# Two pairs of pieces per group in seven products, and four of eight low parts by an accumulating transfer

## The chip, the cores and the metric

One core of one Trainium2 chip runs the whole program. The metric is the device time of one execution in microseconds (us), given as the median of several runs.

## What is computed

Two transformer blocks are applied to 256 tokens of width 2048, all in f32. The change touches only the last stage, the feed-forward of the second block. Cut to that:

```python
hn = rms_norm_2(h, norm_ffn_g)
gate, up = jnp.split(hn @ w_gate_up, 2, axis=-1)     # each 5632 wide
h = h + (jax.nn.silu(gate) * up) @ w_down            # 5632 x 2048
...
return rms_norm_2(h, norm_final_g)
```

## The kernel before

**Pieces.** All weights are streamed from HBM in pieces of two k-tiles of 128 rows by 512 columns (512 KB in SBUF). SyncE loads two pieces with one transfer of 1 MB (L417) into one of four slots of `raw` (`RAWS` = 4). Each f32 weight is split into two parts of type float32r, because a product is made of three: high by high, high by low, low by high. ScalarE rounds the high part into `hi` (L577), VectorE subtracts it from the raw weights and writes the low part into `lo` (L941). `hi` and `lo` have four slots (`RING` = 4). So the split of piece n waits until TensorE has used piece n-4 (`pieces_used`, L574 and L940). In the order of their programs ScalarE and VectorE run three pieces ahead of TensorE (`AHEAD` = 3, `split_to` in `walk`, L496), and there the splits are interleaved with the evacuation of the groups and with other steps. SyncE waits before each load until the low parts of both pieces of the slot are made (`lo_ready`, L405).

**The last stage.** It is written out in three chunks: `f2_up0`, `f2_down0`, `f2_up1`, `f2_down1`, `f2_up2`, `f2_down2` (`ffn`, L134). An up segment computes gate and up products and writes their product, split in two parts, into `B` as tokens (`token_parts`, L368). A down segment multiplies `B` by `w_down` in four groups of 512 output columns. A group has 8 pieces in `f2_down0` and `f2_down1`, and 6 in `f2_down2`. The evacuation of a group (`tpart`, `tlast`, L1170) adds two PSUM banks to the residual `HT`. An ordinary piece of a down group is 12 matmuls of 512 columns (`piece`, L1594, L1616 to L1618).

**Seven products.** In 11 of the 12 down groups pieces 2 and 3 (`SEVEN_AT` = 2, `seven_product_pairs`, L203) are computed by a scheme with seven block products instead of eight: 42 matmuls of 256 columns (`seven_products`, L1751, L1757 to L1759). It needs sums of weight blocks and of activation blocks:

- `block_sums` (L949), in VectorE's program behind the low part of the piece before the pair: four operations, L957 to L961, of which L959 changes the raw weights in place. ScalarE's high part of the pair's first piece waits for it (`t1_set`, L576).
- `t_hi` (ScalarE, L584) and `t_lo` (VectorE, L945), the two parts of the block sums, both behind the split of the pair's second piece.
- `activation_sums` (L976), behind the up group of turn 1 of each up segment (L523): four additions on VectorE (L980 to L983), a copy on ScalarE (L595), a subtraction on VectorE (L987), into `s_form`.
- `combine` (L964): ScalarE copies a product (L589) and VectorE makes five operations (L969 to L974). It runs in the middle of the group, three pieces behind the pair (L520), and adds to `HT`. The group's evacuation (L1174) adds the rest.

GpSimd issues small loads in the first 30 us and nothing after them (L441 to L484).

Of the kernel before, what the change touches and what calls it, by code (L numbers as in the profile page):

```python
# [19 lines left out]
ALU = mybir.AluOpType  # L20
# [25 lines left out]
TOKEN_AT = 16  # L46
# [203 lines left out]
def bass_two_blocks(nc, ins, out):  # L250
    SEGS, TOTAL = schedule()
    PAIRS = seven_product_pairs(SEGS)

    with ExitStack() as ctx:
# [6 lines left out]
        def overlay(**shapes):  # L261
# [19 lines left out]
        s_form, t_sum = overlay(s_form=([P, 2, 4, 2, P], F32R), t_sum=[P, 2, 3, SEVEN_COLS])  # L281
# [8 lines left out]
        small = sb("small", [P, 64])  # L290
        r_fin = sb("r_fin", [P, T])
# [18 lines left out]
        _, t_hi, t_lo = overlay(gfin_end=[P, MT * T + 3 * D], t_hi=([P, 2, 3, SEVEN_COLS], F32R), t_lo=([P, 2, 3, SEVEN_COLS], F32R))  # L310
# [30 lines left out]
            sem("first_block_sums_set"), sem("block_sums_set"), sem("block_sums_hi"), sem("block_sums_lo"), sem("block_sums_used"))  # L341
        s_ready, p1_copied = sem("activation_sums_ready"), sem("first_product_copied")
# [38 lines left out]
        def _(sp):  # L381
# [114 lines left out]
        def walk(eng, tallies, split, evacuate, side, each_turn, combine, activation_sums, last):  # L496
# [5 lines left out]
            for seg in SEGS:  # L502
                def run(turn, t):
# [10 lines left out]
                    for g, kind in enumerate(seg.kinds):  # L514
                        G = turn * len(seg.kinds) + seg.g0 + g
                        for j in range(seg.pieces):
# [3 lines left out]
                            if t is not None and j == SEVEN_AT + 3 and base + g * seg.pieces + SEVEN_AT in PAIRS:  # L520
                                combine(PAIRS[base + g * seg.pieces + SEVEN_AT], b0, turn * len(seg.kinds) + g)
                            if j == seg.pieces - 1:
                                sums = seg.name.startswith("f2_up") and kind == "up" and t == SEVEN_AT // 2  # L523
                                left = [MORE.get(kind, 0) + sums]

                                def more():
# [5 lines left out]
                                         token_parts if seg.name.startswith("f2") else B_parts)  # L532
                                if sums:
                                    activation_sums(more)
# [18 lines left out]
        def _(act):  # L553
# [12 lines left out]
            def split(n, slot):  # L566
# [8 lines left out]
                if isinstance(n, int) and n in PAIRS:  # L575
                    act.wait_ge(t1_set, PAIRS[n] + 1)  # L576
                act.activation(hi[:, slot % RING], raw[:, raw_slot, 2 * (slot % 2):2 * (slot % 2) + 2, :],  # L577
                               ACT.Copy).then_inc(hi_ready, 1)
                if isinstance(n, int) and n - 1 in PAIRS:
                    q = PAIRS[n - 1]  # L580
# [5 lines left out]
            def combine(q, b0, gi):  # L586
# [4 lines left out]
            def activation_sums(more):  # L591
                more()
                asked.skip()
                wait(asked)
                given.mark(act.activation(s_form[:, 0], pb_copy[:, :, :].rearrange("p f (i c) -> p f i c", i=2), ACT.Copy))  # L595
# [25 lines left out]
            def evacuate(kind, G, end, b0, gi, k, more, to_b):  # L621
# [294 lines left out]
            walk(act, {1: asked, 2: given, 3: ready}, split, evacuate, side, lambda quarter, turn: None, combine, activation_sums, last)  # L916
# [3 lines left out]
        def _(dve):  # L920
# [14 lines left out]

            def split(n, slot):

                dve.wait_ge(hi_ready, n + 1)
                if not isinstance(n, int) or n >= RING:
                    dve.wait_ge(pieces_used, n - RING + 1)  # L940
                dve.tensor_tensor(lo[:, slot % RING], raw[:, slot // 2 % RAWS, 2 * (slot % 2):2 * (slot % 2) + 2, :],  # L941
                                  hi[:, slot % RING], ALU.subtract).then_inc(lo_ready, 1)
                if isinstance(n, int) and n - 1 in PAIRS:
                    dve.wait_ge(t_hi_ready, PAIRS[n - 1] + 1)
# [4 lines left out]
            def block_sums(n):  # L949

                w = raw[:, n // 2 % RAWS, :, :].rearrange("p (i e) (s c) -> p i e s c", e=2, s=2)
                dve.wait_ge(raw_landed[n // 2 % RAWS], landed(n // 2))
                dve.wait_ge(h_turned, 16)
                if PAIRS[n]:
                    dve.wait_ge(t_lo_ready, PAIRS[n])
# [6 lines left out]
                dve.wait_ge(t1_set, PAIRS[n] + 1)  # L962

            def combine(q, b0, gi):  # L964

                x = HT[:, :, gi * GC:(gi + 1) * GC]
# [9 lines left out]
            def activation_sums(more):  # L976
# [10 lines left out]
                dve.tensor_tensor(s_form[:, 1], pb_copy[:, :, :].rearrange("p f (i c) -> p f i c", i=2), s_form[:, 0],  # L987
# [32 lines left out]
            def evacuate(kind, G, end, b0, gi, k, more, to_b):  # L1020
# [149 lines left out]
                elif kind in ("tpart", "tlast"):  # L1170
# [3 lines left out]
                    dve.tensor_tensor(x, x, ps[:, b0:b0 + 2, :], ALU.add).then_inc(psum_free, 1)  # L1174
# [343 lines left out]
            walk(dve, {0: own, 1: asked, 2: given, 3: ready}, split, evacuate, side, turn_h, combine, activation_sums, last)  # L1518
# [3 lines left out]
        def _(pe):  # L1522
# [71 lines left out]
            def piece(seg, g, j, slot, b0, n, steps=None):  # L1594
# [3 lines left out]
                if isinstance(n, int) and n == 0:  # L1598
                    pe.wait_ge(first_lo, 1)
                else:  # L1600
                    pe.wait_ge(lo_ready, n + 1)
                for kk in range(2):
                    k = 2 * j + kk + (4 * WIDEST_FIRST[g] if seg.name == "pool" else 0)
                    first = j == 0 and kk == 0
                    final = (j == seg.pieces - 1 or isinstance(n, int) and n == TOTAL - RING - 1) and kk == 1
# [145 lines left out]
            def seven_products(j, slot, b0, n):  # L1751

                Xh, Xl = token_parts
                half = SEVEN_COLS

# [8 lines left out]
                def summed(f, i):  # L1764
                    return s_form[:, 0, f, i, :], s_form[:, 1, f, i, :]
# [9 lines left out]
                pe.wait_ge(s_ready, PAIRS[n] // 4 + 1)  # L1775
                for i in range(2):
                    k = 2 * (j + i)
                    pe.wait_ge(lo_ready, n + i + 1)
                    product(p16[:, 0:half], i == 0, False, tokens(0, k), *block(0, 0, i))
                    product(z0[:, 0:half], False, False, tokens(0, k + 1), *block(1, 0, i))  # L1780
                    product(z0[:, half:GC], False, False, summed(3, i), *block(1, 1, i))
                    product(p57[:, 0:half], i == 0, False, summed(0, i), *block(0, 1, i)).then_inc(pieces_used, 1)
                pe.wait_ge(t_lo_ready, PAIRS[n] + 1)
                for i in range(2):
                    k = 2 * (j + i)
                    product(p16[:, half:GC], False, i == 1, summed(1, i), *block_sum(1, i))
                    product(p57[:, half:GC], False, i == 1, summed(2, i), *block_sum(0, i))
                    last = product(z1[:, 0:half], False, False, tokens(1, k + 1), *block_sum(2, i))
# [24 lines left out]
            for seg in SEGS:  # L1813
                def run(turn, t):
                    for g, kind in enumerate(seg.kinds):
# [10 lines left out]
                        for j in range(seg.pieces - RING if at_end else seg.pieces):  # L1826
# [9 lines left out]
                            if isinstance(n, int) and n in PAIRS:  # L1836
                                seven_products(j, slot, b0, n)
# [47 lines left out]
```

## Time and profile before

| | |
|---|---|
| median of 3 runs | 2616.38 us (2616.24 to 2616.57) |
| the profiled execution, its own time | 2616.46 us |
| its span, first to last instruction | 2614.7 us |
| granted TensorE clock, mean | 0.999 |
| TensorE busy | 2602.3 us, 21534 matmuls |
| VectorE busy, ScalarE busy | 1694.6 us, 1187.4 us |
| DMA, mean over the span | 193 GB/s, 504.31 MB |

Times in the rows are microseconds from the start of the span. PE is TensorE (PEld its weight loads), DVE is VectorE, ACT ScalarE, POOL GpSimd, SP SyncE; a name with q behind it is an engine's queue. L12 is line 12 of the kernel. Matmuls overlap, so the distance between the starts of two matmuls is what one costs, not its own duration.

### The profile page before, as it was taken

What the parts mean: (1) busy time and instruction counts of PE and PEld (TensorE: products, weight loads), DVE (VectorE), ACT (ScalarE), POOL (GpSimd) and SP (SyncE); (2) the same over time, 40 slices, a digit from 0 to 9 for tenths busy, and PEclk for the clock granted to TensorE, in tenths of its full rate; (3) what the DMA queues carried; (4) which work ended last, traced back from release to release, by engine and by line L of the source; (5) the groups of instructions that cost most, each with busy time, mean ns of one, the idle gap of its engine ahead of it and who ended that gap; (6) DMA issues with size and microseconds to landing.
All of it is one profiled execution on the core that took longest, in us unless ns stands there. A gap on an engine that the chain in (4) does not pass through costs nothing.

```text
span 2614.7 us, 50642 instructions
## 1 busy us (share of the span) xinstructions
PE 2602.3 (100%) x21534; PEld 2551.2 (98%) x21534; DVE 1694.6 (65%) x1817; ACT 1187.4 (45%) x1284; POOL 14.6 (1%) x33
## 2 busy tenths in 40 slices
PE   9999999999999999999999999999999999999998
PEld 8989999999999999999999999999999989998997
DVE  7668765555555556795676666556777875677567
ACT  5356554434443444465443433444544444444444
POOL 2000000000000000000000000000000000000000
PEclk9999999999999999999999999999999999999999
DMA  9654566565655565555555555555565555556553
GB/s 306 202 168 163 196 193 196 187 201 187 200 186 200 188 199 193 179 203 195 180 184 189 193 182 190 193 193 194 193 210 194 193 198 193 191 195 205 194 179 129
DMA packets 254461, 504.31 MB, mean 193 GB/s; under 512 B 9390, under 2 KB 11456, under 8 KB 254160
## 3 DMA queue, kind: packets, MB, share of 16 engines
q1 hardware_dynamic: 250160, 496.27, 56.8%
q10 hardware_dynamic: 3136, 4.21, 0.5%
q8 instruction: 131, 2.15, 0.3%
q0 software_dynamic: 992, 1.34, 0.2%
q14 instruction: 42, 0.34, 0.0%
HBM read 498.89 MB, written 2.89 MB: 192 GB/s over the span
## 4 chain that ended last, share of the span: by engine, by line
PE 99%; DVE 1%; issue 0%; ACT 0%; POOL 0%; DVEq 0%; ACTq 0%; POOLq 0%
PE ps L1579 49%; PE ps L1590 25%; PE ps L1637 4%; PE ps L1646 4%; PE ps L1641 3%; PE ps L1616 3%; PE ps L1618 3%; PE ps L1617 3%; PE ps L1757 1%; PE ps L1759 1%; PE ps L1758 1%; PE ps L1626 1%; PE ps L1627 1%; PE ps L1624 1%; DVE lo L941 0%
## 5 line engine op out<-in xcount | busy, mean ns | idle before, releaser
L941 DVE TENSOR_TENSOR lo<-raw,hi 128x1024 fp32r<-128x1024 f32 x939 | 1139.7, 1224 | 792.6 <-ACT hi L577 779.2
L577 ACT ACTIVATE hi<-raw 128x1024 fp32r<-128x1024 f32 x939 | 988.4, 1059 | 1208.0 <-PE ps L1590 924.3
L1579 PE MATMUL ps<-A,hi 128*128 128x256 f32 x7286 | 902.8, 276 | 0.0
L1579 PEld LDWEIGHTS ps<-A,hi 128*128 128x128 f32 x7286 | 861.1, 188 | 0.3
L1579 PE MATMUL ps<-B,hi 128*128 128x256 f32 x3963 | 491.0, 276 | 0.0
L1590 PE MATMUL ps<-A,lo 128*128 128x256 f32 x3648 | 487.7, 276 | 0.0
L1579 PEld LDWEIGHTS ps<-B,hi 128*128 128x128 f32 x3963 | 468.3, 188 | 0.1
L1590 PEld LDWEIGHTS ps<-A,lo 128*128 128x128 f32 x3648 | 447.5, 188 | 0.0
L1590 PE MATMUL ps<-B,lo 128*128 128x256 f32 x1984 | 265.2, 276 | 0.0
L1590 PEld LDWEIGHTS ps<-B,lo 128*128 128x128 f32 x1984 | 243.3, 188 | 0.0
L1637 PE MATMUL ps<-B,hi 128*128 128x260 f32 (+3 forms) x768 | 109.1, 284 | 0.0
L1646 PE MATMUL ps<-B,lo 128*128 128x258 f32 (+3 forms) x768 | 108.7, 284 | 0.0
L1641 PE MATMUL ps<-B,hi 128*128 128x256 f32 x768 | 104.1, 278 | 0.0
L1637 PEld LDWEIGHTS ps<-B,hi 128*128 128x128 f32 x768 | 100.0, 189 | 0.0
L1646 PEld LDWEIGHTS ps<-B,lo 128*128 128x128 f32 x768 | 98.9, 189 | 0.0
L1616 PE MATMUL ps<-hi,B 128*128 128x512 f32 x248 | 96.8, 390 | 0.0
L1618 PE MATMUL ps<-hi,B 128*128 128x512 f32 x248 | 96.6, 389 | 0.0
L1617 PE MATMUL ps<-lo,B 128*128 128x512 f32 x248 | 96.5, 389 | 0.0
L1641 PEld LDWEIGHTS ps<-B,hi 128*128 128x128 f32 x768 | 96.3, 188 | 0.0
L676 ACT ACTIVATE B<-work 128x1024 f32 (+1 forms) x26 | 27.6, 1063 | 72.5 <-DVE work L1081 64.6
L1618 PEld LDWEIGHTS ps<-hi,B 128*128 128x128 f32 x248 | 46.5, 188 | 10.0
L1617 PEld LDWEIGHTS ps<-lo,B 128*128 128x128 f32 x248 | 46.6, 188 | 9.2
(306 smaller groups left out, 1589.5 us busy)
## 6 DMA issues: line engine op xcount, KB each, us to landing
raw<-in_w_in_dram SPq DMA_DIRECT2D x135, 1024.0 KB, 5.1
raw<-in_ffn_w_dram SPq DMA_DIRECT2D x132, 1024.0 KB, 5.1
raw<-in_w_gate_up_dram SPq DMA_DIRECT2D x88, 1024.0 KB, 5.0
raw<-in_w_down_dram SPq DMA_DIRECT2D x44, 1024.0 KB, 5.0
raw<-in_w_out_dram SPq DMA_DIRECT2D x16, 1024.0 KB, 5.1
raw<-in_pl_w_gate_dram SPq DMA_DIRECT2D x16, 1024.0 KB, 5.1
raw<-in_conv_out_w_dram SPq DMA_DIRECT2D x16, 1024.0 KB, 5.0
raw<-in_w_o_dram SPq DMA_DIRECT2D x16, 1024.0 KB, 5.0
```

Source lines behind the costliest of these rows:

```text
L577: act.activation(hi[:, slot % RING], raw[:, raw_slot, 2 * (slot % 2):2 * (slot % 2) + 2, :], ACT.Copy).then_inc(hi_ready, 1)
L676: given.mark(act.activation(some((A_parts if kind == "cb" else to_b)[0], k, 4, 0, T), work[:, :, :], ACT.Copy))
L941: dve.tensor_tensor(lo[:, slot % RING], raw[:, slot // 2 % RAWS, 2 * (slot % 2):2 * (slot % 2) + 2, :], hi[:, slot % RING], ALU.subtract). ...
L1579: pe.matmul(ps[:, b0 + m, 0:T], high(slot, kk, m), x, start=j == 0 and kk == 0 and part == 0, stop=False)
L1590: last = pe.matmul(ps[:, b0 + m, 0:T], low(slot, kk, m), Xh, start=False, stop=j == seg.pieces - 1 and kk == 1)
L1616: pe.matmul(to, Xh, hi[:, slot % RING, kk, :], start=first, stop=False)
L1617: pe.matmul(to, Xh, lo[:, slot % RING, kk, :], start=False, stop=False)
L1618: last = pe.matmul(to, Xl, hi[:, slot % RING, kk, :], start=False, stop=final)
L1624: pe.matmul(to, Wh, Xh, start=first and m % 2 == 0, stop=False, skip_group_check=True)
L1637: pe.matmul(ps[:, b0 + m, 0:with_lo], high(slot, kk, m), B[:, 2 * j + kk, 0:with_lo], start=first and kk == 0, stop=False, skip_group_chec ...
L1641: pe.matmul(ps[:, b0 + m, 0:T], high(slot, kk, m), B_low[:, 2 * j + kk, :], start=False, stop=False, skip_group_check=True)
L1646: last = pe.matmul(ps[:, b0 + m, 0:with_hi], low(slot, kk, m), B[:, 2 * j + kk, 0:with_hi], start=False, stop=final and kk == 1, skip_grou ...
```

## The change

- Pieces 6 and 7 of the 8-piece groups also become a pair in seven products, so that there are 19 pairs instead of 11. The first products of both pairs gather in the same PSUM banks, and `combine` moves from the middle of the group into its evacuation, where it also takes over the addition of the two plain banks.
- The low parts of pieces 0, 1, 4 and 5 of these groups, and of pieces 0 and 1 of the first three groups of `f2_down2`, 38 in all, are no longer made by VectorE. ScalarE writes the negative high part into `lo` with a second activation (scale -1), and GpSimd then issues a transfer that adds the raw weights to it (`accum_op`). TensorE waits for the transfer (`low_landed`), and so does SyncE before it loads over the raw slot.
- `activation_sums` also runs behind the up group of turn 3 in `f2_up0` and `f2_up1`; `s_form` gets a second half.
- Addresses: the tokens in `B` start at column 0 instead of 16, `t_hi` and `t_lo` lie 48 elements further, `t_sum` moves from the place of `h` to another, and `block_sums` no longer waits for `h_turned`.

The diff, cut to its core:

```diff
-TOKEN_AT = 16
+TOKEN_AT = 0
...
-SEVEN_AT = 2
+PAIRS_AT = {"f2_down0": (2, 6), "f2_down1": (2, 6), "f2_down2": (2,)}
+LOWS_BY_DMA_AT = {"f2_down0": (0, 1, 4, 5), "f2_down1": (0, 1, 4, 5), "f2_down2": (0, 1)}
+SUMS_BEHIND = {"f2_up0": (1, 3), "f2_up1": (1, 3), "f2_up2": (1,)}
...
+def down_groups(segs):
+
+
+    return [(x, x.p0 + turn * x.per_turn + g * x.pieces)
+            for x in segs if x.name in PAIRS_AT for turn in range(2) for g in range(2)][:-1]
+
+
 def seven_product_pairs(segs):
 
 
-    first = [x.p0 + turn * x.per_turn + g * x.pieces + SEVEN_AT
-             for x in segs if x.name.startswith("f2_down") for turn in range(2) for g in range(2)]
-    return {n: q for q, n in enumerate(first[:-1])}
+
+    pairs, groups = {}, {}
+    for i, (x, first) in enumerate(down_groups(segs)):
+        for u, j in enumerate(PAIRS_AT[x.name]):
+            pairs[first + j] = (len(pairs), sum(len(PAIRS_AT[f"f2_down{c}"]) for c in range(int(x.name[-1]))) + u, u)
+        groups[first] = (i, len(pairs) - 1)
+    return pairs, groups
+
+
+def lows_by_dma(segs):
+
+
+    count, turns = {}, [0] * RING
+    for x, first in down_groups(segs):
+        for j in LOWS_BY_DMA_AT[x.name]:
+            turns[(first + j) % RING] += 1
+            count[first + j] = turns[(first + j) % RING]
+    return count
...
-        s_form, t_sum = overlay(s_form=([P, 2, 4, 2, P], F32R), t_sum=[P, 2, 3, SEVEN_COLS])
+        s_form, = overlay(s_form=([P, 2, 2, 4, 2, P], F32R))
...
+        t_sum, = overlay(t_sum=[P, 2, 3, SEVEN_COLS])
...
-        _, t_hi, t_lo = overlay(gfin_end=[P, MT * T + 3 * D], t_hi=([P, 2, 3, SEVEN_COLS], F32R), t_lo=([P, 2, 3, SEVEN_COLS], F32R))
+        _, t_hi, t_lo = overlay(gfin_end=[P, MT * T + 3 * D + 48], t_hi=([P, 2, 3, SEVEN_COLS], F32R), t_lo=([P, 2, 3, SEVEN_COLS], F32R))
...
-                                sp.wait_ge(lo_ready, n * 2 - 2 * RAWS + 2)
+                                if isinstance(n, int) and 2 * (n - RAWS) in LOWS_BY_DMA:
+                                    for m in (2 * (n - RAWS), 2 * (n - RAWS) + 1):
+                                        sp.wait_ge(low_landed[m % RING], 16 * LOWS_BY_DMA[m])
+                                else:
+                                    sp.wait_ge(lo_ready, n * 2 - 2 * RAWS + 2)
...
+            for i, n in enumerate(LOWS_BY_DMA):
+                pool.wait_ge(low_begun, i + 1)
+                pool.dma_start(lo[:, n % RING].bitcast(F32), raw[:, n // 2 % RAWS, 2 * (n % 2):2 * (n % 2) + 2, :],
+                               accum_op=ALU.add).then_inc(low_landed[n % RING], 16)
...
-                            if t is not None and j == SEVEN_AT + 3 and base + g * seg.pieces + SEVEN_AT in PAIRS:
-                                combine(PAIRS[base + g * seg.pieces + SEVEN_AT], b0, turn * len(seg.kinds) + g)
                             if j == seg.pieces - 1:
-                                sums = seg.name.startswith("f2_up") and kind == "up" and t == SEVEN_AT // 2
+                                behind = SUMS_BEHIND.get(seg.name, ())
+                                sums = kind == "up" and t in behind
+                                seven = SEVEN_GROUPS.get(base + g * seg.pieces) if t is not None else None
...
                 act.activation(hi[:, slot % RING], raw[:, raw_slot, 2 * (slot % 2):2 * (slot % 2) + 2, :],
                                ACT.Copy).then_inc(hi_ready, 1)
+                if isinstance(n, int) and n in LOWS_BY_DMA:
+                    act.activation(lo[:, slot % RING], raw[:, raw_slot, 2 * (slot % 2):2 * (slot % 2) + 2, :],
+                                   ACT.Copy, scale=-1.0).then_inc(low_begun, 1)
...
-            def evacuate(kind, G, end, b0, gi, k, more, to_b):
+            def evacuate(kind, G, end, b0, gi, k, more, to_b, seven):
+                if seven:
+                    combine(*seven, b0)
...
+                if isinstance(n, int) and n in LOWS_BY_DMA:
+                    passed[0] += 1
+                else:
+                    dve.wait_ge(hi_ready, n + 1)
+                    if not isinstance(n, int) or n >= RING:
+                        dve.wait_ge(pieces_used, n - RING + 1)
+                    dve.tensor_tensor(lo[:, slot % RING], raw[:, slot // 2 % RAWS, 2 * (slot % 2):2 * (slot % 2) + 2, :],
+                                      hi[:, slot % RING], ALU.subtract).then_inc(lo_ready, 1 + passed[0])
+                    passed[0] = 0
...
-                dve.wait_ge(h_turned, 16)
...
+            def combine(c, q, b0, x):
+
                 p1, v5, v7, u2 = (work[:, i, :] for i in range(4))
-                dve.wait_ge(p1_copied, q + 1)
+                dve.wait_ge(t_used, q + 1)
+                own.mark(dve.tensor_tensor(x, x, ps[:, b0:b0 + 2, :], ALU.add))
+                dve.wait_ge(p1_copied, c + 1)
                 step(dve.tensor_tensor(u2, p1, ps[:, b0 + 2, SEVEN_COLS:GC], ALU.add))
                 step(dve.tensor_tensor(work[:, 1:3, :], row_of(u2, 2), ps[:, b0 + 3, :].rearrange("p (s c) -> p s c", s=2), ALU.add))
-                dve.tensor_tensor(x[:, 0, :], x[:, 0, :], work[:, 0:2, :].rearrange("p s c -> p (s c)"), ALU.add)
+                own.mark(dve.tensor_tensor(x[:, 0, :], x[:, 0, :], work[:, 0:2, :].rearrange("p s c -> p (s c)"), ALU.add))
                 x1 = x[:, 1, :].rearrange("p (s c) -> p s c", s=2)
                 step(dve.tensor_tensor(x1, x1, row_of(v7, 2), ALU.add))
-                step(dve.tensor_tensor(x[:, 1, SEVEN_COLS:GC], x[:, 1, SEVEN_COLS:GC], ps[:, b0 + 3, 0:SEVEN_COLS], ALU.add))
-
-            def activation_sums(more):
+                return dve.tensor_tensor(x[:, 1, SEVEN_COLS:GC], x[:, 1, SEVEN_COLS:GC], ps[:, b0 + 3, 0:SEVEN_COLS], ALU.add)
...
+                    if seven:
+                        combine(*seven, b0, x).then_inc(psum_free, 1)
+                    else:
+                        dve.tensor_tensor(x, x, ps[:, b0:b0 + 2, :], ALU.add).then_inc(psum_free, 1)
...
+                elif isinstance(n, int) and n in LOWS_BY_DMA:
+                    pe.wait_ge(low_landed[n % RING], 16 * LOWS_BY_DMA[n])
                 else:
                     pe.wait_ge(lo_ready, n + 1)
...
+                q, sums, u = PAIRS[n]
+                closes = j == seg.pieces - 2
+                last_pair = u == 1 or n + 4 not in PAIRS
...
-                pe.wait_ge(s_ready, PAIRS[n] // 4 + 1)
+                pe.wait_ge(s_ready, sums + 1)
```

## Rows read from the trace of the kernel before

**Rows 1.** The page's first part: busy time of each engine
```profile
PE 2602.3 (100%) x21534; PEld 2551.2 (98%) x21534; DVE 1694.6 (65%) x1817; ACT 1187.4 (45%) x1284; POOL 14.6 (1%) x33
```

**Rows 2.** Whom TensorE waited for, 1900 to 2615 us: total, times, longest
```profile
PE ps L1757 <- DVE lo L941: 2.8, 2, 2.0
```

**Rows 3.** TensorE's timeline, first two groups of f2_down0: start, length, instruction
```profile
2061.39 0.39 PE L1616 MATMUL ps<-hi,B 128*128 128x512 f32 x1
...
2066.85 0.28 PE L1757 MATMUL ps<-hi,B 128*128 128x256 f32 x1
...
2071.77 0.40 PE L1616 MATMUL ps<-hi,B 128*128 128x512 f32 x1
...
2088.13 0.28 PE L1757 MATMUL ps<-hi,B 128*128 128x256 f32 x1
...
2093.05 0.40 PE L1616 MATMUL ps<-hi,B 128*128 128x512 f32 x1
```

**Rows 4.** TensorE's timeline inside the first pair, between which lie four more rows
```profile
2067.56 0.28 PE L1757 MATMUL ps<-hi,s_form 128*128 128x256 f32 x1
...
2068.13 0.28 PE L1759 MATMUL ps<-hi,s_form 128*128 128x256 f32 x1
```

**Rows 5.** ScalarE's timeline, 2050 to 2105 us; in brackets idle time before and releaser
```profile
2053.49 1.06 ACT L577 ACTIVATE hi<-raw 128x1024 fp32r<-128x1024 f32 x1 [1.66 <-PE ps L1590]
...
2067.64 1.06 ACT L676 ACTIVATE B<-work 128x1024 fp32r<-128x1024 f32 x1 [3.55 <-DVE work L1081]
2068.61 3.89 ACT L577 ACTIVATE hi<-raw 128x1024 fp32r<-128x1024 f32 x4
...
2088.39 1.06 ACT L577 ACTIVATE hi<-raw 128x1024 fp32r<-128x1024 f32 x1 [1.41 <-PE ps L1618]
```

**Rows 6.** VectorE's timeline, 2050 to 2105 us
```profile
2068.74 1.23 DVE L1191 TENSOR_TENSOR B<-work,B 128x1024 fp32r<-128x1024 f32 x1 [1.19 <-ACT B L676]
...
2077.02 0.41 DVE L969 TENSOR_TENSOR work<-work,ps 128x256 f32<-128x256 f32 x1
...
2079.98 1.23 DVE L941 TENSOR_TENSOR lo<-raw,hi 128x1024 fp32r<-128x1024 f32 x1
2081.12 0.69 DVE L957 TENSOR_TENSOR t_sum<-raw 128x512 f32<-128x512 f32 x1
...
2083.80 1.23 DVE L941 TENSOR_TENSOR lo<-raw,hi 128x1024 fp32r<-128x1024 f32 x1
...
2087.21 1.75 DVE L945 TENSOR_TENSOR t_lo<-t_sum,t_hi 128x1536 fp32r<-128x1536 f32 x1
2088.88 4.62 DVE L941 TENSOR_TENSOR lo<-raw,hi 128x1024 fp32r<-128x1024 f32 x4
```

**Rows 7.** VectorE's timeline, the activation sums of f2_up0: first addition, what follows the four
```profile
1980.51 0.42 DVE L980 TENSOR_TENSOR pb_copy<-work 128x256 f32<-128x256 f32 x1
...
1982.10 1.22 DVE L941 TENSOR_TENSOR lo<-raw,hi 128x1024 fp32r<-128x1024 f32 x1
```

**Rows 8.** DMA issues: queue, count, KB each, median us from issue to landing
```profile
out_dram<-HT SPq DMA_DIRECT2D x4, 256.0 KB, 3.0
...
ws_in<-in_gmlp_ws_dram POOLq DMA_DIRECT2D x1, 512.0 KB, 7.8
...
relb_in<-in_rel_bias_dram POOLq DMA_DIRECT2D x1, 0.5 KB, 4.9
```

**Rows 9.** Queue of the weights: packets, MB, share of the 16 engines
```profile
q1 hardware_dynamic: 250160, 496.27, 56.8%
```

**Rows 10.** Stretches: length, engines' busy time (instructions), granted clock, DMA share, GB/s
```profile
20.00:25.00 5.00, 5.00 (x28) 4.20 (x27) 4.12 (x6) 2.78 (x6) 2.52 (x5) 1.00 1.06 366
...
2061.39:2146.40 85.01, 85.01 (x458) 73.68 (x457) 70.56 (x75) 40.48 (x41) 0.00 (x0) 1.00 0.56 194
```

**Rows 11.** VectorE's timeline at the first group's end in f2_down2
```profile
2556.97 1.22 DVE L1174 TENSOR_TENSOR HT<-HT,ps 128x1024 f32<-128x1024 f32 x1
2559.60 1.23 DVE L1186 TENSOR_TENSOR HT<-HT,gfin_row 128x1024 f32<-128x1024 f32 x1 [1.40 <-ACT pb_copy L650]
2560.74 1.22 DVE L941 TENSOR_TENSOR lo<-raw,hi 128x1024 fp32r<-128x1024 f32 x1
```

More of the change, by code:

```diff
@@ L341, in bass_two_blocks @@
             sem("first_block_sums_set"), sem("block_sums_set"), sem("block_sums_hi"), sem("block_sums_lo"), sem("block_sums_used"))
+        low_begun, low_landed = sem("negative_high_part_set"), [sem(f"low_part_landed{i}") for i in range(RING)]
         s_ready, p1_copied = sem("activation_sums_ready"), sem("first_product_copied")
@@ L494, in first_tile, with walk @@
             return (turn * len(seg.kinds) + g) * MT
-        def walk(eng, tallies, split, evacuate, side, each_turn, combine, activation_sums, last):
+        def walk(eng, tallies, split, evacuate, side, each_turn, activation_sums, last):
             at = {"split": AHEAD}
@@ L531, in run @@
                                 evacuate(kind, G, end, b0, turn * len(seg.kinds) + g, first_tile(seg, turn, g), more,
-                                         token_parts if seg.name.startswith("f2") else B_parts)
+                                         token_parts if seg.name.startswith("f2") else B_parts, seven)
                                 if sums:
-                                    activation_sums(more)
+                                    activation_sums(more, behind.index(t))
                                 assert left[0] == 0, (kind, left)
@@ L589, in combine, with activation_sums @@
                 act.activation(work[:, 0, :], ps[:, b0 + 2, 0:SEVEN_COLS], ACT.Copy).then_inc(p1_copied, 1)
-            def activation_sums(more):
+            def activation_sums(more, u):
                 more()
@@ L914, in last @@
                         act.dma_start(out[0, a * P:(a + 1) * P, c:e], HT[:, a, c:e]).then_inc(stored, 16)
-            walk(act, {1: asked, 2: given, 3: ready}, split, evacuate, side, lambda quarter, turn: None, combine, activation_sums, last)
+            walk(act, {1: asked, 2: given, 3: ready}, split, evacuate, side, lambda quarter, turn: None, activation_sums, last)
         @block.vector
@@ L1018, in residual_out, with evacuate @@
                 ready.mark(dve.tensor_tensor(some(A, k, 4, T, 2 * T), hk, some(A, k, 4, 0, T), ALU.subtract))
-            def evacuate(kind, G, end, b0, gi, k, more, to_b):
+            def evacuate(kind, G, end, b0, gi, k, more, to_b, seven):
                 Rm = row_of(R, MT)
@@ L1516, in last @@
                         dve.tensor_scalar(HT[:, a, c:e], HT[:, a, c:e], r, None, ALU.mult).then_inc(left_scaled, 1)
-            walk(dve, {0: own, 1: asked, 2: given, 3: ready}, split, evacuate, side, turn_h, combine, activation_sums, last)
+            walk(dve, {0: own, 1: asked, 2: given, 3: ready}, split, evacuate, side, turn_h, activation_sums, last)
         @block.tensor
@@ L1604, in piece @@
                     first = j == 0 and kk == 0
-                    final = (j == seg.pieces - 1 or isinstance(n, int) and n == TOTAL - RING - 1) and kk == 1
+                    final = (j == seg.pieces - 1 or isinstance(n, int) and n + 1 in PAIRS and j == seg.pieces - 3 or isinstance(n, int) and n == TOTAL - RING - 1) and kk == 1
                     if layout == "token":
@@ L1778, in seven_products @@
                     pe.wait_ge(lo_ready, n + i + 1)
[L1779 to L1783, printed above, removed]
+                    product(p16[:, 0:half], u == 0 and i == 0, False, tokens(0, k), *block(0, 0, i))
+                    product(z0[:, 0:half], False, closes and i == 1, tokens(0, k + 1), *block(1, 0, i))
+                    product(z0[:, half:GC], False, closes and i == 1, summed(3, i), *block(1, 1, i))
+                    product(p57[:, 0:half], u == 0 and i == 0, False, summed(0, i), *block(0, 1, i)).then_inc(pieces_used, 1)
+                pe.wait_ge(t_lo_ready, q + 1)
                 for i in range(2):
                     k = 2 * (j + i)
-                    product(p16[:, half:GC], False, i == 1, summed(1, i), *block_sum(1, i))
-                    product(p57[:, half:GC], False, i == 1, summed(2, i), *block_sum(0, i))
-                    last = product(z1[:, 0:half], False, False, tokens(1, k + 1), *block_sum(2, i))
+                    product(p16[:, half:GC], False, last_pair and i == 1, summed(1, i), *block_sum(1, i))
+                    product(p57[:, half:GC], False, last_pair and i == 1, summed(2, i), *block_sum(0, i))
+                    last = product(z1[:, 0:half], False, closes and i == 1, tokens(1, k + 1), *block_sum(2, i))
                 last.then_inc(t_used, 1)
```

39 lines of the change are left out of this document (17 added, 22 removed).

## The prediction

> **What bounds the kernel now.** I read the page's busy times first: TensorE is busy for 2602.3 of 2614.7 us [rows 1], so only fewer or cheaper matmuls make it faster, and any new wait of TensorE is paid in full. Then its waits: in the last 715 us it waited 2.8 us for low parts in seven-product pairs [rows 2]. Then its timeline in the stage that changes: the group period of `f2_down0` is 2093.05 - 2071.77 = 21.28 us, and its pair takes 2071.77 - 2066.85 = 4.92 us; six ordinary pieces take 2088.13 - 2071.77 = 16.36 us, 2.73 each [rows 3]. Two ordinary pieces are 5.45 us, so a pair saves 0.53. Last I read the two helpers there, because the change moves work between them and puts GpSimd's transfers on the path.
>
> **The gain.** 19 - 11 = 8 more pairs at 0.53 us: -4.3 us.
>
> **The helpers' totals.** In an 8-piece group VectorE loses four low parts of 1.14 us (2081.12 - 2079.98), 4.6 us, and gains four block sums, 2083.80 - 2081.12 = 2.68, and one `t_lo`, 2088.88 - 2087.21 = 1.67, together 4.35 [rows 6]: no change. ScalarE gains four negative copies of 0.97 (3.89 for four) and one more `t_hi`, and was under half busy in these 85 us [rows 5, 10]. Both are cover, cost 0. If it went, the order at a group's end would be paid: VectorE now has 1.14 for the plain banks (2.96 for the rest of `combine` [rows 6]), 4.1 us in one run that starts 0.26 us behind the group's last matmul. Then come the low part of piece 3, ready at 5.5 us and needed at 5.45 + 1.4 = 6.85 (half of the pair's first phase), and `t_lo`, ready at 7.2 and needed at 8.25. Cost 0, with 1.0 us of cover; ScalarE's copy, high part and `t_hi` (0.37, 0.97, 1.4 us) lie beside it.
>
> **The new wait: how much time the transfer has.** Piece 4's slot is free when TensorE starts piece 1. In the trace a high part starts 0.26 us behind such a point (2088.39 against 2088.13) [rows 3, 5]; the high part to the next takes 0.97 and the negative copy 1.06, so the transfer can be issued at 2.29. Piece 4 is needed after piece 1 and a pair, 2.73 + 4.92 = 7.65 us. Less 0.15 us for two semaphore steps (an estimate) the transfer has 5.2 us. Pieces 5, 0 and 1 of the next group have the same 7.65 us. A wait at the first of two pieces gives the second the same time, so each couple pays once: L - 5.2, where L is the time from issue to landing. In `f2_down0` and `f2_down1` there are 12 such couples. The first couple of each down segment has more: high part at 2053.49, piece 0 at 2061.39, so 5.7 us; three of them. The two later ones of `f2_down2` (piece 2 of the pair frees the slot) have 6.5 us.
>
> **The first group of `f2_down0` and `f2_down1`.** There ScalarE is late already: it waits for VectorE before its copy into `B` at 2067.64, and the high part of piece 4 follows at 2068.61, where piece 4 starts at 2071.77 [rows 3, 5]. With two low parts off VectorE I take this chain 0.6 us earlier; then the negative copy ends near 2070.1, and piece 4 waits until 2070.2 + L. Piece 5 is later still, because `activation_sums` now stands here between the two: VectorE's copy into `B`, at 2068.74 less 0.6, plus 1.14, four additions 1.6 (1982.10 - 1980.51), ScalarE's copy 1.06, high part and negative copy 2.03: 2074.0 [rows 6, 7]. That is 3.9 us behind piece 4's, and piece 4 itself takes 2.73, so another 1.2 to 1.3 us. Per group: (L - 1.6) + 1.3, twice.
>
> **The size of L.** No row shows an accumulating transfer, so it is bounded. From below: SyncE's store of 256 KB lands in 3.0 us near the end [rows 8]; the weights' queue moved 496.27 MB in 56.8% of 2614.7 us, 334 GB/s [rows 9], so another 256 KB is 0.8 us, and GpSimd's issuing some tenths: 4.0. From above: GpSimd's own transfer of the same 512 KB took 7.8 us [rows 8], at a DMA share of 1.06 [rows 10]; an accumulation reads two operands, another 512 KB at 334 GB/s, 1.5 us: 9.3. I take the two rows by the DMA share here, 0.56 [rows 10]: 4.0 + 0.56 x 3.8 = 6.1 us. Even the 0.5 KB transfer of this queue took 4.9 us [rows 8].
>
> The Trainium skill ("DMA: Bandwidth & Descriptors", Anatomy of one DMA) fits a GpSimd transfer by about 2.0 us and bytes over 436 GB/s, which would be an estimate of 3.2 us. The row of 7.8 us speaks against it beside a full load; by it the sum would be +1.5 us, which lies inside the first rival below.
>
> **The rest.** Addresses: inside the pair the `s_form` matmuls stand (2068.13 - 2067.56)/5 = 0.114 us apart, against 4.92/42 = 0.117 for all [rows 3, 4]; if the moved buffers brought all to 0.1135, it would be 0.15 us a pair, -2.9 in 19. I take 0, and 0 as the other end. The stalls of `f2_down2`: in the first group's end the low part of piece 3 came at 2560.74 + 1.22, behind the addition, ScalarE's squares and the gain (3.77 from 2556.97 to 2560.74) [rows 11]. Now the 2.96 of `combine` stand behind the group's end, but the run starts at once: 0.26 + 2.96 + 3.77 + 1.22 = 8.2 against 6.85, 1.35 us in each of two groups, 2.7 for the 2.8 of [rows 2]: 0, between -2.8 and +1. SyncE now waits for landed low parts, up to 6 us later than before; the weights are needed about a group later, cost 0. GpSimd's queue is empty otherwise, and its waits hold nobody else.
>
> **The sum** at L = 6.1: pairs -4.3; 12 couples x 0.9 = +10.8; two first groups x 5.8 = +11.6; three first couples x 0.4 = +1.2. Together +19.3 us on the profiled execution's 2616.46 (0.08 above the median of the runs): 2635.8. At L = 4.0: -4.3 + 2 x 3.7 = +3.1. At 7.8: -4.3 + 31.2 + 15.0 + 6.3 + 2.6 = +50.8. At 9.3: +79.
>
> **Rivals.** What a measurement can tell from no change is taken as 0.2%, 5.2 us.
>
> *The transfers land in time.* L is at most 5.0, because there is room on the DMA engines; then the 12 couples cost nothing, only the first groups' 2 x 4.7 stand against -4.3, +5.1 at L = 5 and +3.1 at L = 4. The address term could take 2.9 more. It gives 2614 to 2621, middle 2619: no change. Chance 0.27.
>
> *Faster.* As above, and the first groups' chain is not as late as I hold, since ScalarE's copy into `B` comes down with VectorE's load: then -4.3, up to -2.9 for the addresses and up to -2.8 for the stalls. It decides at L below 5.2 and piece 4 of the first group hardly waiting; 2609. [Rows 5] speak against it: ScalarE finished that high part at best 2.1 us before piece 4 started. Chance 0.15.
>
> *The DMA engines become the bound.* A group loads 4 MB, at 334 GB/s 12.6 us of 20.8. Four accumulations that read two operands of 512 KB are another 12.6, 25.2 in all: the group would take 25.2 instead of 21.28, +3.9 in each of eight, 31, with the first groups' waits +43: 2659. Chance 0.13. The Trainium skill ("Collectives: The Full Stack", The bandwidth ceiling) says that an add in the DMA engines costs by its two source reads, twice the read traffic; no run here shows it.
>
> **Numbers.** The forecast, slower by late low parts, has 0.45 (its own range 2622 to 2667). With the DMA bound slower has 0.58, the same 0.27, faster 0.15. The range leaves out faster and the top beyond L = 7.8: 2612 to 2666.
>
> **What would show it.** Right: TensorE waits of about 1 us in front of pieces 0 and 4 of the down groups, released by DMA; 4 to 5 us at piece 4 of the first group in `f2_down0` and `f2_down1`, and about 1 us at piece 5; 19 pairs of 4.9 us; issue to landing near 6 us; the DMA share in the groups up from 0.56. Wrong: transfers that land within 5 us; pairs near 4.8; waits for VectorE at the pairs' second piece in `f2_down0`, which would mean that `combine` at the group's end is not covered; or weights that come late.

## The result, and the profile after

The changed kernel takes 2672.64 us (median of 4 runs, 2662.82 to 2675.31) against 2616.40 of the kernel before: a ratio of 1.0208, 95% interval 1.0191 to 1.0225, or 56 us slower. The profiled execution took 2671.48 us, its span is 2669.7 us, 55.0 more than before. The prediction said slower, but 2635.8 us, and at most 2666.

The page after: engines' busy time, the queues' packets, MB and share of the 16 DMA engines, and the chain that ended last.

```profile
span 2669.7 us, 51047 instructions
PE 2622.3 (98%) x21678; PEld 2570.3 (96%) x21678; DVE 1693.6 (63%) x1829; ACT 1237.0 (46%) x1332; POOL 47.2 (2%) x71
...
q1 hardware_dynamic: 250160, 496.27, 55.9%
q0 software_dynamic: 6464, 21.26, 4.0%
...
PE 93%; DMA 4%; ACT 1%; DVE 1%; issue 1%; POOL 0%; DVEq 0%; ACTq 0%; POOLq 0%
```

TensorE no longer stands nearly alone in the chain: the transfers, which had no part in it before, have 4%. VectorE is as busy as before [rows 1], as forecast. Now TensorE's waits (total, times, longest), and GpSimd's transfers (count, KB, median from issue to landing; then the spread):

```profile
PE ps L1669 <- DMA lo<-raw: 36.6, 13, 4.7
...
PE ps L1861 <- DVE lo L987: 1.0, 1, 1.0
PE ps L1813 <- DVE lo L987: 1.0, 1, 1.0
...
lo<-raw POOLq DMA_DIRECT2D x38, 512.0 KB, 6.6
...
DMA to landing us min/median/max: 4.5/6.6/9.7
```

**Where the 55 us went.** Each stretch runs from the start of its first matmul to the start of the next stretch's first (the last one to the end of the span). The usual distances between matmuls (0.2267 us for 512 columns, 0.1133 for 256) divide the excess: a distance with idle time in it is a wait, and another that is over 30% too long is put down to the lower clock. Counted by distance, a wait is some 0.16 us longer than the idle time that the views give.

| stretch | before | after | more |
|---|---|---|---|
| f2_down0 | 85.14 | 106.99 | 21.9: waits 18.7, lower clock 5.8 |
| f2_up1 | 174.57 | 181.34 | 6.8: each matmul a little dearer |
| f2_down1 | 85.13 | 108.70 | 23.6: waits 16.4, lower clock 8.9 |
| f2_up2 | 130.94 | 130.91 | 0.0 |
| f2_down2 and the end | 77.51 | 80.43 | 2.9: waits 6.0 (4.1 before), lower clock 3.1 (2.4) |

In the two down segments with 8-piece groups, waits and clock are 49.8 us where there were none. Less the forecast 4.3 for the pairs that is 45.5, and 45.4 were found.

**Two waits, followed back.** The rows come from the timelines of the changed kernel's engines (start, length, engine, instruction; in brackets the idle time before and its releaser). In order of time they show: a transfer's issue on GpSimd (POOL) and TensorE's piece behind it, then SyncE's loads, ScalarE's negative copy, the next transfer and the piece behind that.

```profile
2070.30 0.85 POOL L519 DMA_DIRECT2D lo<-raw  x1 [10.98 <-ACT lo L616]
...
2074.97 0.76 PE L1669 MATMUL ps<-hi,B 128*128 128x512 f32 x1 [3.24 <-DMA lo<-raw]
...
2078.79 0.92 SPq L448 DMA_DIRECT2D raw<-in_w_down_dram  x2
...
2080.45 1.04 ACT L616 ACTIVATE lo<-raw 128x1024 fp32r<-128x1024 f32 x1
...
2081.79 0.85 POOL L519 DMA_DIRECT2D lo<-raw  x1 [6.71 <-ACT lo L616]
...
2090.11 0.47 PE L1669 MATMUL ps<-hi,B 128*128 128x512 f32 x1 [3.03 <-DMA lo<-raw]
```

The transfer of 2070.30 has the DMA engines nearly to itself (the last load lands 0.7 us after its issue), and TensorE goes on 4.7 us later. The one of 2081.79 takes 8.3 us, since SyncE has issued two loads of 1 MB back to back at 2078.79. They were let go by the landing of the couple before it (its second transfer landed at 2078.73), and so they stand in the way of the next couple. SyncE's waits, 2050 to 2170 us, show the same dependence (total, times, longest):

```profile
SPq L434 <- DMA lo<-raw: 99.9, 8, 14.3
```

The packets recorded in the trace show how the loads delay the transfer. The first packet of the transfer of 2070.30 starts 1.42 us after the issue. That of 2081.79 starts 4.35 us after it, at 2086.14, when the loads' packets are nearly through (the last ends at 2087.14). From its first packet to its landing the one takes 3.1 us and the other 3.8. So 2.9 of the 3.6 us more are spent before the transfer begins to move.

The DMA share, first in stretches of 2 us (length, GpSimd's busy time, granted clock, DMA share, GB/s), then over the whole of `f2_down0` (there with the busy times of all engines):

```profile
2072.00:2074.00 2.00, 0.00 (x0) 1.00 1.06 203
2074.00:2076.00 2.00, 0.85 (x1) 0.66 0.39 74
2076.00:2078.00 2.00, 0.00 (x0) 0.50 1.06 203
...
2082.00:2084.00 2.00, 0.64 (x1) 1.00 1.05 408
...
2086.00:2088.00 2.00, 0.00 (x0) 1.00 1.05 239
2088.00:2090.00 2.00, 0.00 (x0) 1.00 1.09 215
...
2061.32:2168.31 106.99, 89.25 (x530) 78.66 (x529) 72.02 (x81) 60.14 (x59) 11.94 (x14) 0.94 0.84 230
```

An accumulating transfer fills the engines (1.06) at 203 GB/s; where the loads run, the same share moves 408. The share of the whole stretch is 0.84 (0.56 before [rows 10]), but in the wait that ends at 2090.11 it is over 1 (1.05 and 1.09).

**The lower clock.** The same stretch shows a granted clock of 0.50, the lower of the two levels, 1.2 of 2.4 GHz, right behind TensorE's wait of 3.24 us. The matmuls there start 0.43 us apart instead of 0.23:

```profile
2075.96 0.63 PE L1671 MATMUL ps<-hi,B 128*128 128x512 f32 x1
2076.39 0.63 PE L1669 MATMUL ps<-hi,B 128*128 128x512 f32 x1
2076.82 0.63 PE L1670 MATMUL ps<-lo,B 128*128 128x512 f32 x1
```

### The profile page after: what moved, and what is told of

Read it like the earlier page. It is cut to its first block, busy times and chain, and to the rows that moved or that the text cites. A ratio compares the mean times of both kernels' runs of the same rounds, so it can differ in the third digit from the quotient of the medians.

```text
span 2669.7 us, 51047 instructions
## 1 busy us (share of the span) xinstructions
PE 2622.3 (98%) x21678; PEld 2570.3 (96%) x21678; DVE 1693.6 (63%) x1829; ACT 1237.0 (46%) x1332; POOL 47.2 (2%) x71
## 4 chain that ended last, share of the span: by engine, by line
PE 93%; DMA 4%; ACT 1%; DVE 1%; issue 1%; POOL 0%; DVEq 0%; ACTq 0%; POOLq 0%
PE ps L1630 48%; PE ps L1641 24%; DMA lo<-raw 4%; PE ps L1690 4%; PE ps L1699 3%; PE ps L1694 3%; PE ps L1669 2%; PE ps L1671 2%; PE ps L1670 2%; ACT hi L613 1%; PE ps L1680 1%; PE ps L1679 1%; PE ps L1677 1%; ACT lo L616 0%; PE ps L1813 0%
## 5 line engine op out<-in xcount | busy, mean ns | idle before, releaser
L987 DVE TENSOR_TENSOR lo<-raw,hi 128x1024 fp32r<-128x1024 f32 x901 | 1095.1, 1224 | 831.9 <-ACT hi L613 819.1
L1669 PE MATMUL ps<-hi,B 128*128 128x512 f32 x184 | 80.5, 438 | 36.6 <-DMA lo<-raw 36.6
L1669 PEld LDWEIGHTS ps<-hi,B 128*128 128x128 f32 x184 | 38.4, 209 | 48.0 <-issue 28.8
L1670 PE MATMUL ps<-lo,B 128*128 128x512 f32 x184 | 78.1, 424 | 0.0
L1671 PE MATMUL ps<-hi,B 128*128 128x512 f32 x184 | 77.9, 424 | 0.0
L519 POOL DMA_DIRECT2D lo<-raw x38 | 32.6, 857 | 2562.8 <-ACT lo L616 2562.8
```

The source lines that it names most:

```text
L519: pool.dma_start(lo[:, n % RING].bitcast(F32), raw[:, n // 2 % RAWS, 2 * (n % 2):2 * (n % 2) + 2, :], accum_op=ALU.add).then_inc(low_lande ...
L1669: pe.matmul(to, Xh, hi[:, slot % RING, kk, :], start=first, stop=False)
L1670: pe.matmul(to, Xh, lo[:, slot % RING, kk, :], start=False, stop=False)
L1671: last = pe.matmul(to, Xl, hi[:, slot % RING, kk, :], start=False, stop=final)
```

## The experiments

**Undoing one part at a time.** Four kernels from the changed one. In c SyncE's wait changes in the same way as TensorE's; in d both also wait for the high part, which now comes last. The edits, cut to their core:

```diff
# a_lows_by_vectore
-LOWS_BY_DMA_AT = {"f2_down0": (0, 1, 4, 5), "f2_down1": (0, 1, 4, 5), "f2_down2": (0, 1)}
+LOWS_BY_DMA_AT = {"f2_down0": (), "f2_down1": (), "f2_down2": ()}
# b_one_pair
-PAIRS_AT = {"f2_down0": (2, 6), "f2_down1": (2, 6), "f2_down2": (2,)}
+PAIRS_AT = {"f2_down0": (2,), "f2_down1": (2,), "f2_down2": (2,)}
-SUMS_BEHIND = {"f2_up0": (1, 3), "f2_up1": (1, 3), "f2_up2": (1,)}
+SUMS_BEHIND = {"f2_up0": (1,), "f2_up1": (1,), "f2_up2": (1,)}
# c_no_transfer (TensorE and SyncE)
-pool.dma_start(lo[:, n % RING].bitcast(F32), ...)
-pe.wait_ge(low_landed[n % RING], 16 * LOWS_BY_DMA[n])
+pe.wait_ge(low_begun, list(LOWS_BY_DMA).index(n) + 1)
...
# d_negative_first
+act.activation(lo[...], raw[...], ACT.Copy, scale=-1.0)   # ahead of the high part
 act.activation(hi[...], raw[...], ACT.Copy)
-act.activation(lo[...], raw[...], ACT.Copy, scale=-1.0)
...
```

> The changed kernel with all low parts by VectorE again and no accumulating transfer; two pairs per group and the combination at the group's end stay. Theory (the late transfers are the loss): the waits for DMA go. VectorE then needs 17.4 + 4.6 = 22 us of work in a group of 20.8 us, so it costs about 1 us in each of eight groups: 2614 to 2630 us. Rival (the second pair and the combination at the group's end are the loss): 2650 us or more.

> The changed kernel with one pair per group (pieces 2 and 3) and one activation sum per up segment, but with the 38 accumulating transfers. Theory: nearly the whole loss stays, 2655 to 2680 us, since the transfers for pieces 4 and 5 have the same 5.2 us and those for 0 and 1 only 0.5 us more. Rival (second pair and combination): near 2620 us.

> The changed kernel without the transfers themselves: ScalarE still writes the negative high part, and TensorE and SyncE wait for that; the low parts of 38 pieces are left out of the computation. Theory: 2612 to 2622 us, -4 us for the pairs and up to +7 us for the slower matmuls of the second up segment, if those belong to the changed order of matmuls and not to the transfers. Rival (the second activation on ScalarE is the loss): 2640 us or more.

> The changed kernel with the negative copy ahead of the high part, so that each transfer is issued 0.97 us earlier. If the transfer's time is a fixed latency, each of about 14 waits is 1 us shorter, and some lowered clocks go: 2645 to 2660 us. If what counts is the collision with the weight loads, which start when the couple before has landed, the gain is less than 5 us or spread irregularly: 2665 to 2675 us.

| kernel | median us | ratio to before, interval |
|---|---|---|
| a_lows_by_vectore | 2635.72 | 1.0074, 1.0057 to 1.0091 |
| b_one_pair | 2672.71 | 1.0215, 1.0194 to 1.0235 |
| c_no_transfer | 2623.27 | 1.0025, 1.0016 to 1.0035 |
| d_negative_first | 2666.20 | 1.0190, 1.0167 to 1.0212 |

With the transfers and without the second pair (b) the whole loss is there. Without the transfers (c) `f2_down0` takes 83.33 us, 1.8 less than before. So the transfers are the loss in the down segments, not the second pair, the combination at the group's end or ScalarE's second activation. Kernel a lies above its range, and c 1.3 us above its own. In part a's loss is VectorE, whose low parts TensorE awaits for 11.0 us in all, against 3.6 in the kernel before (total, times, longest):

```profile
PE ps L1813 <- DVE lo L987: 8.5, 8, 1.9
PE ps L1669 <- DVE lo L987: 1.5, 2, 1.0
PE ps L1861 <- DVE lo L987: 1.0, 1, 1.0
```

With these waits and the lower clock behind two of them, a's two 8-piece segments take 89.76 and 89.46 us, 8.9 more than before: without the transfers the second pairs are a loss too, though a smaller one.

The rest is in the up segments: 181.34 us for `f2_up1` in a and c alike, and 136.0 for `f2_up2` instead of 130.9. That is 11.8 us that belong neither to pairs nor to transfers. Kernel d can issue each transfer about 1 us earlier, and its two 8-piece segments took 106.56 and 110.82 us, as long as before (106.99 and 108.70). Its transfers took longer instead, median 8.0 us:

```profile
DMA to landing us min/median/max: 4.5/8.0/10.5
```

A fixed latency would have given each wait 1 us back. Instead the total stayed (38.9 us of waits for DMA), as the collision with the loads would have it.

**What a transfer costs, and what it collides with.**

```diff
# e_plain_copy
-pool.dma_start(lo[...], raw[...], accum_op=ALU.add).then_inc(low_landed[n % RING], 16)
+pool.dma_start(lo[...], raw[...]).then_inc(low_landed[n % RING], 16)
# f_half_loads
-sp.dma_start(raw[:, slot, :, :], weights(name)[:, k:k + 4, ...])
+m = 2 if seg.name.startswith("f2_down") else 4
+sp.dma_start(raw[:, slot, 0:m, :], weights(name)[:, k:k + m, ...])
```

> The changed kernel with the 38 transfers as plain copies, nothing added (the low parts of these pieces are left out of the computation, the bytes, queue and waits are the same). If the addition costs by its second operand, a lone transfer falls from 4.5 us to about 3.5, a colliding one from 8 to 9 us to about 6, and the kernel to 2630 to 2650 us. Rival (the queue's own latency is the cost, whatever it does with the data): no change, 2665 to 2680 us.

> The changed kernel with weight loads of half the bytes in the three down segments (the other half of those weights is left out of the computation). Theory (the transfers are late because they collide with two weight loads issued back to back): issue to landing falls to 5 to 6 us, the waits for DMA to less than half of 37 us, and the time to 2625 to 2650 us. Rival (a transfer's time does not depend on the loads): 2665 to 2680 us.

The plain copy: 2646.51 us, ratio 1.0115 (1.0098 to 1.0131), within its range; the waits for DMA fall from 36.6 to 19.9 us. Its queue's row, and issue to landing:

```profile
q0 software_dynamic: 6464, 21.26, 2.0%
...
DMA to landing us min/median/max: 2.8/4.5/8.9
```

The same packets and bytes take half the share, 2.0% instead of 4.0. Less the 0.2% that this queue has in kernel a for the small loads of the start, one accumulating transfer takes (4.0 - 0.2)% of 2669.7 us over 38, 2.7 us of all 16 engines, and a plain one 1.25. So the addition costs about as much as a second transfer of the same bytes. With half the load bytes the kernel takes 2655.45 us (1.0140, 1.0124 to 1.0157), just above its range. The median from issue to landing falls to 5.3 us, as expected; the waits fall from 36.6 to 23.8 us, and not to less than half:

```profile
PE ps L1670 <- DMA lo<-raw: 23.8, 12, 3.6
...
DMA to landing us min/median/max: 4.5/5.3/9.4
```

Both halves of the cause are seen: the transfer's own 4.5 us at the least, and the loads beside it. Neither alone is all.

**The dearer matmuls of the up segments.**

```diff
# g_addresses (from the kernel before)
-TOKEN_AT = 16
+TOKEN_AT = 0
-        _, t_hi, t_lo = overlay(gfin_end=[P, MT * T + 3 * D], ...)
+        _, t_hi, t_lo = overlay(gfin_end=[P, MT * T + 3 * D + 48], ...)
# h_steps (from c_no_transfer); k_before_cut (from the kernel before); l_changed_cut (from the changed one)
-EVERY_TURN = {("f2_up1", 0): (0, 248), ("f2_up2", 0): (0, 248), ...}
+EVERY_TURN = {("f2_up1", 0): (0, P), ("f2_up2", 0): (0, P), ...}
```

The last line is one that the change did not touch: it cuts one matmul at the start of each turn of an up segment into two, of 248 and 8 columns.

> The kernel before with only two addresses of the change: the tokens in B at column 0, and the block sums' parts 48 elements further. If the slower matmuls of f2_up1 (0.1175 us apart instead of 0.1131) come from the addresses: 2623 to 2629 us. If they come from the changed order of matmuls in the down segments: 2616 us within 1 us, or up to 2 us less when the pairs get cheaper.

> The kernel without transfers (as c_no_transfer) with the split matmul at the start of f2_up1 and f2_up2 cut at 128 columns instead of 248. If the distance of the matmuls is a state that such a cut sets: one or both segments fall back to 0.1131 us a matmul, 2611 to 2618 us. Rival (the distance is fixed by addresses): 2623 us as before.

> The kernel before with the cut at 128 instead of 248 columns in f2_up1 and f2_up2. If 128 is the right cut whatever came before: 2616 us. If the cut that gives 0.1131 us a matmul depends on the addresses in use: 0.1175 us in one or both segments, 2621 to 2628 us.

> The changed kernel with the cut at 128 columns. f2_up1 loses its 6.8 us, f2_up2 stays at 130.9 us: 2665 us, with the waits of the down segments as they were. If the state after a stall differs from run to run: 2665 to 2675 us, with f2_up1 or f2_up2 slow in the profile.

| kernel | median us | ratio | f2_up1, f2_up2 us |
|---|---|---|---|
| g_addresses | 2627.44 | 1.0043, 1.0026 to 1.0059 | 181.33, 136.01 |
| h_steps | 2612.11 | 0.9984, 0.9975 to 0.9994 | 174.60, 130.95 |
| k_before_cut | 2616.18 | 1.0000, 0.9991 to 1.0009 | 174.61, 130.97 |
| l_changed_cut | 2663.52 | 1.0185, 1.0171 to 1.0199 | 174.81, 130.95 |

The two addresses alone cost 11 us, in segments whose matmuls read neither buffer. With the new addresses, a cut at 128 columns took it back wherever it was tried (h, l, and i, j, m and n below). The stretch 2150 to 2300 us in g and in h: length, TensorE's busy time (matmuls), and so on, granted clock, DMA share, GB/s:

```profile
2150.00:2300.00 150.00, 150.00 (x1276) 150.00 (x1275) 81.47 (x70) 63.09 (x60) 0.00 (x0) 1.00 0.57 187
...
2150.00:2300.00 150.00, 150.00 (x1326) 150.00 (x1325) 86.16 (x75) 65.10 (x63) 0.00 (x0) 1.00 0.59 197
```

The clock is 1.00 in both, and TensorE is never idle; it just starts 1276 matmuls in one and 1326 in the other. In each trace one of two distances (0.1177 or 0.1133 us) holds from a segment's start to its end. The addresses and the cut don't settle alone which: in the profiled execution of d, with the new addresses and the old cut, `f2_up1` was fast (175.83 us, with a wait of 1.1 at its end) and `f2_up2` slow (136.00), the other way round from the changed kernel. The executions of c_no_transfer spread over 2617.67 to 2624.14 us, so it may also differ between executions; what in the machine it is was not found.

**Is the lower clock a consequence of the waits?** In l_changed_cut TensorE was kept busy in front of the first transfer of each couple, except at a segment's start:

```diff
# m_filler
+if j in (0, 4) and n != seg.p0:
...
+    for _ in range(14):
+        pe.matmul(ps[:, ...], X[0][:, 2 * j, 0:P], hi[:, slot % RING, 0, :], start=True, stop=True)
 pe.wait_ge(low_landed[n % RING], 16 * LOWS_BY_DMA[n])
```

> l_changed_cut with 14 more matmuls of 512 columns (3.2 us, their results are overwritten) ahead of each wait for the first transfer of a couple, except at the start of a segment. If the idle time of TensorE brings the lower clock: the granted clock is 1.00, the stretches at 0.43 us a matmul (some 16 us in all) go, the waits shrink to what is over 3.2 us, and the filler costs up to 5 us where a wait was shorter: 2644 to 2656 us. If the clock falls for another reason in these stages: the stretches stay, 2663 to 2675 us.

Measured 2669.11 us (1.0202, 1.0187 to 1.0218), so the time was missed, but not the question. The whole of `f2_down0` and two stretches of 2 us (length, busy times of all engines, granted clock, DMA share, GB/s):

```profile
2061.61:2172.16 110.55, 107.18 (x628) 92.47 (x627) 72.02 (x81) 60.07 (x59) 11.95 (x14) 1.00 0.82 223
2074.00:2076.00 2.00, 2.00 (x10) 1.38 (x9) 1.93 (x4) 1.19 (x2) 0.85 (x1) 1.00 0.36 68
2076.00:2078.00 2.00, 2.00 (x10) 1.47 (x8) 1.95 (x3) 2.00 (x3) 0.00 (x0) 1.00 1.10 209
```

The granted clock is 1.00 where it was 0.66 and 0.50, with the same transfers in flight. So the lower clock comes from TensorE's idle time and not from the transfers. The time was missed by simple counting: sixteen fillers of 14 x 0.227 = 3.2 us are 51 us, while all waits and overlong distances in the three down segments were 58 us in l_changed_cut and are still 11 here.

**Looking for a faster kernel.** i takes transfers for pieces 0 and 1 alone, d's order and the cut; j and n make all low parts on VectorE, and give the second pair only to groups with time for it:

```diff
# j_three_groups, n_two_groups: no transfers, the cut, and
-        for u, j in enumerate(PAIRS_AT[x.name]):
+        for u, j in enumerate(PAIRS_AT[x.name] if first != x.p0 else PAIRS_AT[x.name][:1]):            # j
+        for u, j in enumerate(PAIRS_AT[x.name] if (first - x.p0) // x.pieces % 2 else PAIRS_AT[x.name][:1]):   # n
                                 if sums:
+                                    if behind.index(t) == 1:
+                                        split_to(at["split"] + 2)
```

> The changed kernel with transfers for pieces 0 and 1 alone (22 of 38), the low parts of 4 and 5 by VectorE, the negative copy first, and the cut of h_steps. The loads are then no longer let go in twos by a landed couple. If collisions make the transfers late: issue to landing 5 to 6.5 us against 6.2 us of time, few short waits, VectorE at 19.7 us in a group of 20.8 us: 2612 to 2622 us. If a couple is late for its own reasons: eleven waits of 2 us and more, 2635 us or more.

> An attempt at a faster kernel: the changed one with no transfers, the second pair only in groups 1 to 3 of f2_down0 and f2_down1, the second activation sums two splits later, and the cut of h_steps. The pairs give 6 x 0.53 = 3.2 us, the waits for VectorE of a_lows_by_vectore (8.5 us) go in part: 2612 to 2619 us. If VectorE's 22 us in such a group are paid in full: 2620 us or more.

> As j_three_groups, with the second pair only in groups 1 and 3 of f2_down0 and f2_down1. If VectorE has time for a second pair in every other group (39.5 us of work in two groups of 42 us): 4 x 0.53 = 2.1 us less and no new waits, 2613.5 to 2615.5 us. If a group with two pairs is late by itself: 2616 us or more.

Kernel i: 2634.13 us (1.0069, 1.0056 to 1.0083), above its range and next to what late couples would give. The loads no longer come in twos from a landing, but at least one load is still on its way at each transfer's issue or follows it within 1 us, and a transfer takes 5.5 us at the least:

```profile
DMA to landing us min/median/max: 5.5/7.0/9.9
...
PE ps L1671 <- DMA lo<-raw: 17.6, 8, 6.4
```

Kernel j: 2616.27 us (1.0000, 0.9991 to 1.0009): three second pairs in four groups give what VectorE's waits take. Kernel n, with two in four: 2614.71 us (11 runs, 2614.57 to 2615.12) against 2616.37 (15 runs, 2615.80 to 2616.79), ratio 0.9994, interval 0.9985 to 1.0003. The runs don't overlap, but a gain of 1.7 us is less than the interval can tell. It is the best version found; none clearly beats the kernel before.

## Why the prediction was right and wrong

**The direction and its mechanism** were right: late low parts by transfer, in front of pieces 0 and 4, dearer in each segment's first group. So were the costs put at nothing for the helpers' totals and for the combination at the group's end: in the 8-piece segments no piece waited for VectorE. The pairs' -4.3 us stands nearly: it fits the balance above, and in c the two 8-piece segments together are 3.6 us shorter. That h_steps, the change without transfers and dear matmuls, is 4.2 us under the kernel before is in part luck, as 1.7 of it lie in `f2_down2`, which gained no pair. The 5.2 us that a transfer was to have came out as well: of the transfer of 2081.79, the piece was due 5.1 us behind the issue.

**Three terms failed.** The forecast was +19.3 us, and the spans differ by 55.0. Of these 36 us some 13 are longer waits, some 15 the lower clock and 7 the addresses.

**The size of L, the term that was mis-sized.** I took 4.0 + 0.56 x 3.8 = 6.1 us. The bounds of 4.0 and 9.3 held nearly (4.5 to 9.7). That the median of all (6.6) is close is luck, since it lies between two kinds of transfer. A mean DMA share says nothing of the moments that count. The transfers are issued just behind loads that a landing couple set free, and those that TensorE waited for in the later groups mostly took 8 us and more (7 of 10). I had followed SyncE's new wait for what it does to the weights, "cost 0", and not for what its loads then collide with. For the 12 couples I forecast 0.9 us each, 10.8; ten of them waited, 27.0 us in all, and two not at all. All waits together: forecast 23.6 us, measured 36.6.

**The lower clock, a step that was missing.** I priced a wait at its own length. No term of the sum stood for what follows a wait. In the two segments 35.1 us of waits brought 14.7 us more for matmuls at the lower clock with them, and m_filler shows that it is the idle time that brings it. Rows of the kernel before had it too: behind its waits in `f2_down2` it lost 2.4 us that way.

**The addresses.** "I take 0, and 0 as the other end" was wrong on the other end. I looked at the pairs alone, and the cost came in the up segments: 6.8 us in this program, 11 in the old kernel.

**The first groups** came out as worked: 3.24 us at piece 4 with 4.7 us from issue to matmul, where L - 1.6 is 3.1. Piece 5 did not wait, because piece 4 ran at the lower clock; that cost about the same (1.5 us against the 1.3 of the forecast). The first couples of the segments did not wait (forecast 1.2), and one of `f2_down2`, taken as free, waited 3.5.

**The rivals.** "In time" and "faster" were wrong. The DMA bound (2659) is nearest in number, and its premise of two operands holds: 2.7 us of all engines for a transfer against the 3.1 assumed. The Trainium skill ("Collectives: The Full Stack", The bandwidth ceiling) says that an add costs by its two source reads. This case's trace agrees in size, 4.0% of the engines' time against 2.0, though it can't tell the second read from the adding. But the share stayed at 0.84, so not bandwidth over the group but waiting on each transfer set the time. The estimate of 3.2 us from the fit in the Trainium skill ("DMA: Bandwidth & Descriptors", Anatomy of one DMA) lies near the shortest plain copy, 2.8; the shortest accumulating one was 4.5, so the fit doesn't cover the addition.

## What to carry to other kernels

Price a transfer on the critical path by the moment of its issue: which loads its own predecessor sets free, and what the queue shows while they run, not the mean share. Add to TensorE's waits the stretches at the lower clock behind them, here 0.4 us for each microsecond waited. And when buffers move, look at the matmul distance of stages that don't use them: here 0.1177 against 0.1133 us was worth more than the change could gain.

## What was not expected of the hardware

- An accumulating transfer of 512 KB between SBUF buffers takes 2.7 us of all 16 engines and at least 4.5 us from issue to landing; a plain one 1.25 and 2.8.
- Matmuls of 256 columns run at one of two distances, 0.1133 or 0.1177 us, at a granted clock of 1.00 and without idle time. Moving two buffers changed it for 300 us; cutting one matmul in each turn at 128 instead of 248 columns changed it back. Kernel d, fast in one of the two segments and slow in the other, shows that more than these two settle it.
- The transfer that was issued 3 us behind two loads of 1 MB moved nothing until these were nearly through: its first packet started 4.35 us after the issue, against 1.42 for the one that had the engines to itself.
- TensorE's clock fell to the lower level late in or just behind 8 of the 10 waits of over 2 us (at that of 3.24 us above it did, at that of 3.03 us it did not), and its matmuls ran there for 3 to 6 us. A shorter wait can be enough: behind waits of 1.86 us in a and 1.99 in the kernel before it fell too. With matmuls in the waits it did not fall.
